# A hybrid decoder step: stacked 16-bit products for the sample states, and the query accumulator read before the decay exponentials

## The reference, cut to what matters

```python
# hgrn2_block, for the sample tokens of one sequence (c = 4)
b = jnp.cumsum(log_f, axis=1)
b_last = b[:, -1]
s_new = jnp.exp(b_last)[..., None] * s0 + jnp.einsum('bshk,bshv->bhkv', k * jnp.exp(b_last[:, None] - b), v)
# retention_block
s_new = jnp.exp(c * log_gamma)[None, :, None, None] * s0 + jnp.einsum('bshk,bshv->bhkv', k * k_dec[None, :, :, None], v)
```

## Time and profile before

| | |
|---|---|
| median of 3 runs | 1737.02 us |
| the profiled execution | 1742.57 us |
| its span on the core | 1741.0 us |
| TensorE busy | 1567.8 us, 90% of the span |
| VectorE busy | 904.5 us, 52% |
| ScalarE busy | 654.0 us, 38% |
| GpSimd busy | 154.3 us, 9% |
| mean granted TensorE clock | 0.931 of full speed |

### The profile page before, as it was taken

One profiled execution on the slowest core, in us unless ns is written; L12 is line 12 of the kernel. 1 busy time (PEld: TensorE's weight loads), 2 busy tenths in 40 slices (PEclk: granted clock), 3 DMA queues, 4 the chain that ended last, 5 costly groups with the idle time before them and its releaser, 6 DMA issues.

```text
span 1741.0 us, 31399 instructions
## 1 busy us (share of the span) xinstructions
PE 1567.8 (90%) x12107; PEld 1251.0 (72%) x12107; DVE 904.5 (52%) x1389; ACT 654.0 (38%) x920; POOL 154.3 (9%) x126
## 2 busy tenths in 40 slices
PE   4699999989699999999867999999886999999994
PEld 3477777767578888788755777777765888887883
DVE  4766644444565555533266665444356555553334
ACT  3645523332353334422155452333225443333213
POOL 2111111100200000000030111000002000000002
PEclk8799989988899999999978899999888999999997
DMA  6132222221123332233221224232031223322321
GB/s 192 46 90 77 75 75 75 74 74 55 57 73 97 96 96 77 70 93 95 82 66 51 74 74 111 57 88 78 27 97 48 88 83 96 96 81 74 97 66 51
DMA packets 175035, 138.05 MB, mean 79 GB/s; under 512 B 5064, under 2 KB 169192, under 8 KB 174776
## 3 DMA queue, kind: packets, MB, share of 16 engines
q1 hardware_dynamic: 168192, 113.46, 22.0%
q0 software_dynamic: 5408, 18.60, 3.8%
q10 hardware_dynamic: 1372, 5.16, 0.9%
HBM read 125.12 MB, written 12.07 MB: 79 GB/s over the span
## 4 chain that ended last, share of the span: by engine, by line
PE 77%; DVE 9%; ACT 6%; issue 4%; DVEq 2%; ACTq 1%; DMA 1%; SPq 0%
PE ACC L510 61%; PE SCR L624 2%; PE OT L632 2%; PE SCR L662 1%; ACT WH L830 1%; DVE X L1193 1%; PE OT L684 1%; PE SCR L545 1%; PE SCR L727 1%; DVE Z L1222 1%; DVE Fb L1206 1%; DVE WL L1153 1%; PE OT L600 1%; DVEq L1261 1%; PE OT L599 1%
## 5 line engine op out<-in xcount | busy, mean ns | idle before, releaser
L510 PE MATMUL ACC<-XH,WH 128*128 128x280 f16 x2432 | 502.6, 289 | 70.8 <-DVE XL L1196 43.1
L510 PE MATMUL ACC<-XL,WH 128*128 128x280 f16 x2432 | 502.4, 289 | 0.0
L510 PE MATMUL ACC<-XH,WL 128*128 128x280 f16 x2432 | 501.6, 289 | 0.0
L510 PEld LDWEIGHTS ACC<-XH,WH 128*128 128x128 f16 x2432 | 238.7, 101 | 153.0 <-DVE XL L1196 45.6
L1153 DVE SCALAR_TENSOR_TENSOR WL<-stage,WH 128x2048 f16<-128x2048 f32 (+1 forms) x116 | 245.9, 2120 | 182.0 <-ACT WH L830 170.2
L510 PEld LDWEIGHTS ACC<-XL,WH 128*128 128x128 f16 x2432 | 243.3, 100 | 58.6
L510 PEld LDWEIGHTS ACC<-XH,WL 128*128 128x128 f16 x2432 | 243.3, 100 | 58.0
L830 ACT ACTIVATE WH<-stage 128x2048 f16<-128x2048 f32 (+1 forms) x116 | 204.8, 1766 | 103.7 <-PE ACC L510 86.9
L510 PE MATMUL ACC<-shared,WH 128*128 128x280 f16 x1408 | 225.2, 283 | 0.2
L510 PEld LDWEIGHTS ACC<-shared,WH 128*128 128x128 f16 x1408 | 137.6, 98 | 30.8 <-issue 0.8
L510 PE MATMUL ACC<-shared,WL 128*128 128x280 f16 x704 | 141.5, 283 | 0.0
(11 more groups left out here) (238 smaller groups left out, 1791.4 us busy)
## 6 DMA issues: line engine op xcount, KB each, us to landing
stage<-in_w_in_dram SPq DMA_DIRECT2D x64, 512.0 KB, 5.3
stage<-in_w_a_dram SPq DMA_DIRECT2D x44, 512.0 KB, 4.3
stage<-in_w_b_dram SPq DMA_DIRECT2D x44, 512.0 KB, 4.8
stage<-in_w_down_dram SPq DMA_DIRECT2D x32, 384.0 KB, 3.3
stage<-in_w_down_dram SPq DMA_DIRECT2D x32, 320.0 KB, 3.7
out_dram<-shared POOLq DMA_DIRECT2D x16, 512.0 KB, 3.9
stage<-in_w_o_dram SPq DMA_DIRECT2D x16, 512.0 KB, 3.9
shared<-in_state_hgrn_dram POOLq DMA_DIRECT2D x8, 512.0 KB, 5.7
```

Source lines behind the costliest of these rows:

```text
L510: last = mm(ACC[:, acc, h, 0:HALF], lhs, x[:, xk + k, h * HALF:(h + 1) * HALF], start=begin, stop=end)
```

## The change

The product `KVTS` by `VX` becomes one float16 product over 96 rows in place of a float32 product over 32. The 96 rows are three stacked copies of the 32 sample tokens. The keys are stacked as high, high, low, and the values as high, low, high, so that the sum over 96 rows gives the same three products as the large matmuls do.

- The sample columns of `KE` and `V` are stored three times, so one transpose of 96 columns gives three copies: VectorE copies `KE` (`twice`, one more instruction of 64 elements in `hg_query` and in `rt_query`), ScalarE reads the accumulator a second time for `V` (64 elements).
- ScalarE copies the 96 rows out of PSUM twice, as float16 (`KV3`) and as float32 (`KVF`), ahead of `tok_ready`: one more instruction of 256 elements for an HGRN head, two more of 128 for a retention head.
- VectorE makes the two low blocks by subtraction (`low_sample_rows`, two instructions on 32 rows by 128), between a wait for `tok_ready` and a new semaphore `kv_low`. It stands right after L1202 in an HGRN gate, ahead of `rt_key` in the group of HGRN head 3, and for retention heads after all scores have been read (after L1394 and its drain, ahead of L1153).
- GpSimd's `VX` waits for `kv_low` in place of `tok_ready`. It has 96 rows and float16 operands, with 1024 elements per row as before.
- ScalarE reads the query accumulator ahead of the decay exponentials in all HGRN groups. VectorE still clamps and uses the query in the same place of its order.

```diff
+TS3 = 3 * TS
...
-        VX = sb("VX", [TS, DEC_BATCH, P])
-        KVTS = sb("KVTS", [TS, 2, P])
+        VX = sb("VX", [TS3, DEC_BATCH, P], F16)
+        KV3 = sb("KV3", [TS3, 2, P], F16)
+        KVF = sb("KVF", [TS3, 2, P])
...
-                pool.wait_ge(tok_ready, hh + 1)
-                nc.gpsimd.tensor_tensor(VX[:, :, :], KVTS[:, 1:2, :].to_broadcast([TS, DEC_BATCH, P]), bcast(seqm[0:TS, :], P),
+                pool.wait_ge(kv_low, hh + 1)
+                nc.gpsimd.tensor_tensor(VX[:, :, :], KV3[:, 1:2, :].to_broadcast([TS3, DEC_BATCH, P]), bcast(seqm[0:TS3, :], P),
                                         ALU.mult).then_inc(vx_ready, 1)
...
-                            last = nc.tensor.transpose(SCR[0:TS, bank, i * P:(i + 1) * P], src[:, TP:T], ident)
+                            last = nc.tensor.transpose(SCR[0:TS3, bank, i * P:(i + 1) * P], src[:, TP:TP + TS3], ident)
...
-                mm(SCR[:, bank, :], KVTS[:, 0, :], VX[:, 4 * n:4 * n + 4, :].rearrange("p b v -> p (b v)"),
+                mm(SCR[:, bank, :], KV3[:, 0, :], VX[:, 4 * n:4 * n + 4, :].rearrange("p b v -> p (b v)"),
                    start=True, stop=True).then_inc(scr_full, 1)
...
-                f(halves(buf[:, 0:T]), ACC[:, c, :, 0:HALF], ACT.Copy, scale=INV_W).then_inc(acc_read[c], 1)
+                last = f(halves(buf[:, 0:T]), ACC[:, c, :, 0:HALF], ACT.Copy, scale=INV_W)
+                if buf is V:
+                    last = f(twice(V), ACC[:, c, 1:2, HALF - TS:HALF].to_broadcast([P, 2, TS]), ACT.Copy, scale=INV_W)
+                last.then_inc(acc_read[c], 1)
...
-                f(KVTS[:, :, :], SCR[0:TS, 0, 0:2 * P].rearrange("p (n v) -> p n v", n=2), ACT.Copy).then_inc(scr_read[0], 1)
+                f(KV3[:, :, :], SCR[0:TS3, 0, 0:2 * P].rearrange("p (n v) -> p n v", n=2), ACT.Copy)
+                f(KVF[:, :, :], SCR[0:TS3, 0, 0:2 * P].rearrange("p (n v) -> p n v", n=2), ACT.Copy).then_inc(scr_read[0], 1)
                 act.drain().then_inc(tok_ready, 1)
...
-                f(KVTS[:, 0, :], SCR[0:TS, 0, 2 * P:3 * P], ACT.Copy, scale=tab[0:TS, ds(cols["k_dec_s"][0] + p, 1)])
-                f(KVTS[:, 1, :], SCR[0:TS, 0, 3 * P:4 * P], ACT.Copy).then_inc(scr_read[0], 1)
+                for rows_ in (KV3, KVF):
+                    f(rows_[:, 0, :], SCR[0:TS3, 0, 2 * P:3 * P], ACT.Copy, scale=tab[0:TS3, ds(cols["k_dec_s"][0] + p, 1)])
+                    last = f(rows_[:, 1, :], SCR[0:TS3, 0, 3 * P:4 * P], ACT.Copy)
+                last.then_inc(scr_read[0], 1)
...
-                    if d is None:
-                        read_acc(Q, 1, tile + 1, None)
+                    read_acc(Q, 1, tile + 1, None)
                     hg_exponentials(l, head)
-                    if d is not None:
-                        read_acc(Q, 1, tile + 1, None)
...
+            def low_sample_rows(hh):
+
+                dve.wait_ge(tok_ready, hh + 1)
+                for n, rows_ in enumerate((slice(2 * TS, TS3), slice(TS, 2 * TS))):
+                    tt(KV3[rows_, n, :], KVF[rows_, n, :], KV3[rows_, n, :], ALU.subtract)
+                dve.drain().then_inc(kv_low, 1)
...
                 dve.drain().then_inc(f_ready, 1)
+                if low_rows is not None:
+                    low_rows()
...
+                nc.vector.tensor_copy(twice(KE), KE[:, TP:T].unsqueeze(1).to_broadcast([P, 2, TS]))
                 dve.drain().then_inc(ew_ready, 1)
...
                 dve.drain().then_inc(pts_ready, 1)
+                low_sample_rows(hh)
...
                     if after_hgrn:
 
+                        hgrn_rows()
                         dve.wait_ge(tok_ready, hh)
                     rt_key(tile)
```

More of the change, by code:

```diff
@@ L143, in const_tables @@
     put("mask32", causal)
-    put("seq", tok[:, None] // DEC_SEQ == np.arange(DEC_BATCH)[None, :])
+    put("seq", np.tile(tok[:, None] // DEC_SEQ == np.arange(DEC_BATCH)[None, :], (3, 1)))
     log_g = np.log1p(-np.exp2(-5.0 - np.arange(HEADS)))
@@ L154, in const_tables @@
     put("k_dec", np.where(left >= 0, np.exp(np.maximum(left, 0) * log_g[None, None, :]), 0.0) * root)
-    put("k_dec_s", np.exp((DEC_SEQ - 1 - tok % DEC_SEQ)[:, None] * log_g[None, :]) * root)
+    put("k_dec_s", np.tile(np.exp((DEC_SEQ - 1 - tok % DEC_SEQ)[:, None] * log_g[None, :]) * root, (3, 1)))
     put("gamma4", np.broadcast_to(np.exp(DEC_SEQ * log_g), (P, HEADS)))
@@ L218, in hybrid_decoder_step @@
         Fb, T1, T2, T3, B, Q, QS, QD, KE, E, V, G = (
-            sb(n, [P, T + 2]) for n in ("Fb", "T1", "T2", "T3", "B", "Q", "QS", "QD", "KE", "E", "V", "G"))
+            sb(n, [P, T + (2 * TS if n in ("KE", "V") else 2)]) for n in ("Fb", "T1", "T2", "T3", "B", "Q", "QS", "QD", "KE", "E", "V", "G"))
         at = [0]
@@ L291, in hybrid_decoder_step @@
         tok_ready, vx_ready, pts_ready, states_ready = sem("tok_ready"), sem("vx_ready"), sem("pts_ready"), sem("states_ready")
+        kv_low = sem("kv_low")
         decays_used = sem("decays_used")
@@ L328, in bcast, with twice @@
             return ap.unsqueeze(2).to_broadcast([ap.shape[0], ap.shape[1], n])
+        def twice(t):
+            return t[:, T:T + 2 * TS].rearrange("p (a t) -> p a t", a=2)
         def level_halves(n, src=None):
@@ L629, in sample_output @@
                 cols_ = OT[:, 1, TP - SPLIT:REST]
-                mm(cols_, KVTS[:, 1, :], PTSS[:, :], start=True, stop=False, skip_group_check=True)
+                mm(cols_, KVF[0:TS, 1, :], PTSS[:, :], start=True, stop=False, skip_group_check=True)
                 for b in range(DEC_BATCH):
@@ L653, in rest_transposes @@
                         nc.tensor.transpose(SCR[0:TAIL, 0, n * P:(n + 1) * P], src[:, 4 * P:TP], ident)
-                        last = nc.tensor.transpose(SCR[0:TS, 0, (2 + n) * P:(3 + n) * P], src[:, TP:T], ident)
+                        last = nc.tensor.transpose(SCR[0:TS3, 0, (2 + n) * P:(3 + n) * P], src[:, TP:TP + TS3], ident)
                     last.then_inc(scr_full, 1)
@@ L1196, in norm_apply, with hg_gate @@
                         tt(XL[:, m - 2, :], X[:, m - 2, :], XH[:, m - 2, :], ALU.subtract).then_inc(x_ready, 1)
-            def hg_gate(l, p, tile):
+            def low_sample_rows(hh):
[3 more added lines that the diff above has]
+                dve.drain().then_inc(kv_low, 1)
+            def hg_gate(l, p, tile, low_rows=None):
                 n = l * HEADS + p
@@ L1436, in group @@
                 split_lo(1, j)
+                hgrn_rows = (lambda: low_sample_rows(hh - 1)) if steps else None
                 if kind == 0:
-                    hg_gate(l, head, tile)
+                    hg_gate(l, head, tile, hgrn_rows)
                     hg_exponents(l, head)
```

## The result

The changed kernel takes 1728.3 us (median of 6 runs, 1724.82 to 1733.6), the kernel before, run beside it, 1737.76 (6 runs, 1736.96 to 1739.92). The ratio is 0.9945 with a 95% interval of 0.9928 to 0.9963: faster by about 9.5 us. The forecast was 1728.8.

A forecast was written before the change was run, and what follows sets the result against it. TensorE, busy for 90% of the span, was taken as the bound, where it isn't waiting for another engine right after. Heads -4.8 us and clock -3.4 gave -8.2: 1737.0 to 1728.8 us, range 1719 to 1740.

The forecast's parts named there:

- The saving of 20 us in all: Sample product on TensorE: 1.72 us falls to 0.44, 1.28 saved in each of 16 heads, at full clock.
- Second copy: ScalarE's extra read ahead of `tok_ready` in an HGRN head: 0.3 us.
- Low rows: VectorE's two subtractions ahead of `VX`: 0.28 us each, 0.48 together, overlapping by 0.08.
- L624's slip: HGRN heads: the sample product starts 1.0 us later because `VX` does; bounds 0.6 and 1.3.
- the sign: Expected in the profile after, HGRN heads: L1206 at 2.5 us or more, or L1207 stretched.
- the slow and the fast `VX`: Rivals on GpSimd's float16 `VX`: slow, above 1740 us in all, chance 0.06; fast at 1.4, about 1721, 0.08.
- The port: A VectorE instruction with two SBUF inputs stands still until GpSimd's is over; L1206 takes 2.19 us, 0.73 elsewhere.
- The retention heads: `VX` goes ahead of L1153: heads 0 and 1 -0.35 us each, head 2 -0.9, head 3 +0.2.
- tip over at 0.1: Port order rival, retention heads: L1153 issued under 0.1 us after the drain goes before `VX`; 1742 us, chance 0.07.
- The query read: ScalarE's earlier read of 0.6 us in HGRN heads goes into a gap: no gain and no loss.
- the term: Clock gain at HGRN head 3: half-clock stretch shortens from 6.8 to 3.4 us, 1.7 won per layer, -3.4 in all.
- the forecast's own sign of being wrong: Wrong if `VX` has another length, L1153 comes first, or half-clock stretches move in heads 1 and 2.

The follow-up runs named there:

- e3: Changed kernel with second copy, low rows and later `VX` kept, but the product again float32 over 32 rows: 1770.6 us, ratio 1.0189.
- e1: Kernel before with only the query read moved ahead of the decay exponentials: 1739.45 us, ratio 1.0002.
- e5: Changed kernel with GpSimd's decay of the HGRN states moved ahead of `VX`: 1705.91 us, ratio 0.9813.
- e10: Kernel before with only GpSimd's decay moved ahead of `VX`: 1723.48 us, ratio 0.9913.
- e9: Changed kernel with GpSimd computing `VX` twice, the second giving the signal: 1787.27 us, ratio 1.0278.
- e4: Changed kernel without the two low-row subtractions and their drain, `VX` released by `tok_ready`; a price only: 1714.94 us, ratio 0.9855.
- e7: Changed kernel with the moves of e5 and e6 together: 1698.48 us, ratio 0.9771.
- e2: Changed kernel with the query read put back behind the decay exponentials: 1730.0 us, ratio 0.9955.
- e8: Changed kernel with the retention heads' low rows moved behind L1163, so VectorE has the port first: 1753.36 us, ratio 1.0089.
- e6: Changed kernel with the retention heads' low rows moved behind the second mask job, among the score reads: 1726.31 us, ratio 0.9937.

## Why the forecast came out right

**The product.** Forecast: 32 instructions for 64, 0.22 us start to start, 96 rows free. The trace shows 32 of L631, and at full clock TensorE's next work starts 0.22 us after L631's start in retention head 1 (309.67 after 309.45). The saving of 20 us in all measured 16.9 (e3 against the change, at full clock).

**What stands ahead of `VX`.** Second copy 0.3, measured 0.28. Low rows 0.48, measured 0.58: the overlap with each other was too generous. Drain and answer 0.13, measured 0.11. The sum of 1.0 for L624's slip came out as 0.9 (wait 3.38 for 2.45). HGRN heads 1 and 2 change by +0.1, as forecast (in both layers against e1): the start slips by 0.9 where 1.0 was put, and the product is 0.8 shorter where 0.9 was put. L1225 takes 2.84 us, over the 2.5 that was named as the sign.

**`VX` itself.** 1.89 was taken and 1.887 is there; the slow and the fast `VX` are out. The Trainium skill, page "GPSIMD Engine Reference", section "Elementwise — side-by-side cycle accounting", counts elements and not bytes, and the trace agrees on that; its estimate of 2.2 us is 0.3 too long here.

**The port.** L1206's 2.19 was read as a wait for GpSimd, and e5 and e10 show that: with GpSimd's second instruction elsewhere it is 0.97 and 0.74. The Trainium skill, page "SBUF — State Buffer", section "Who interferes with whom", has it that whoever issues first holds the port for its whole instruction. The trace agrees for L1163's 3.88 (forecast 4.2) and e9's 3.83: each is one's own time and the other's rest. It doesn't tell who goes next where both have an instruction ready: L1225 was issued before L430 and came after it.

**The retention heads.** Their order, `VX` ahead of L1163, was right, and its margin in the trace is 0.15 us (307.43, 307.58), where the forecast had it tip over at 0.1. TensorE waits 0.45 for `VX` (0.35 forecast) in head 1, 1.09 in head 3 (1.4 by the forecast's times), and 0.37 at slot 16. In sum -1.0 and -1.3 per layer against -1.4. Single heads differ by more (head 0 of layer 0 +0.9 against -0.35, head 2 -1.8 against -0.9), with half-clock stretches at other places than before; which of them makes which difference I didn't settle.

**The query read.** Nothing, as forecast (e1).

**The clock.** Where the term was applied, its size held: head 3's stretch went from 6.8 us to 3.4 at 230.0, and the head gained 2.4 us in both layers where -2.6 was forecast. Heads 1 and 2 of layer 0 kept their 3.4 us (at 154.7 and 195.6), so the forecast's own sign of being wrong did not come up there. But in layer 0 the 3.4 us came back behind head 3 (below), so the gain that was counted for that layer is not a net one.

Over both layers the profiles of e1 and of the changed kernel give the best comparison. The heads have 78.5 us at half clock in e1 and 71.7 in the changed kernel, all of the difference in layer 1. By the estimate of full clock their 7.4 us are 3.4 of clock and 4.0 of work and waits, where the forecast had 3.4 and 4.8. Against the profile of the kernel before, with two long stretches more in heads 0 and 1 of layer 1, they are 10.6.

What the forecast left at nothing is the clock outside the heads: 4.9 us between these two profiles, 4.1 between those of before and after. A stretch of 3.4 us between 18 and 20 stands in the profiles of before, e3, e4, e7 and e10 and not in the others, so it doesn't go with the product. The time at half clock behind the last head is 52.2 us in e1 too, and 45.9 in e2; why it differs stays open. So the mechanism and the parts by head came out, with the work and waits somewhat too large and the clock as a whole too small (8.3 us in the pair with e1, 11.7 in the pair with the kernel before, 3.4 forecast). That the total came to within 0.5 us of the median, when six runs of the changed kernel spread over 9 us, is luck.

**The windows of the changed kernel** at head 3's stretch, and one that is new behind it (before, 3.4 us at 248):

```profile
230.00:233.40 3.40, 3.40 (x16) 2.10 (x15) 2.47 (x4) 1.91 (x1) 0.90 (x2) 0.53 0.06 19
243.00:249.80 6.80, 5.50 (x21) 3.79 (x22) 2.27 (x5) 0.68 (x3) 0.62 (x1) 0.53 0.31 77
```

So a stretch that is shortened at one place can come back at another, here behind the head's sample output; no run tells what decides that.

## What to carry to other kernels

Before work is taken off the busiest engine, look at what the new form asks of the others ahead of it: here 17 us of shorter products were bought with 14 us of longer waits (at full clock), and it was the order on GpSimd, untouched by the change, that was worth most (15 us alone, and 22 on top of the change). When a VectorE instruction takes three times what it takes elsewhere, look for a GpSimd instruction that ends just before it does, and move that, not the VectorE work. One profile of each kernel is not enough to assign the time head by head: here a second profile with the old product (e1) took away 3.3 us that had looked like the change's. And a wait of TensorE is priced twice, once for itself and once for the half clock that may follow: 13.9 and 15.6 us in e3, 3.0 and 23.8 in e8, but 4.9 won and 3.3 lost in e6, so the second price has to be measured.

## What the runs showed of the hardware

- GpSimd and VectorE can take turns at the port when each has one instruction right behind the other: in e9's HGRN head 1 a 0.73 us update (L1229) takes 2.45 us between a `VX` of 2.28 and a decay of 2.42. They need not: in the changed kernel's head 1 the waiting update comes after both GpSimd instructions and takes 2.84.
- A `tensor_scalar` on VectorE is held up too: L1424, 1024 elements, takes 2.23 us behind `VX` in retention head 3 of the changed kernel, and 0.75 where GpSimd is idle.
- At almost the same wait ahead of it, the kind of product (four float32 instructions or two float16) decided between 6.8 and 3.4 us at half clock in HGRN head 1, and with a wait of 1.50 the float16 product was followed by none.
- GpSimd's elementwise product takes the same 1.89 us for 96 partitions of float16 as for 32 of float32.
